# Layer 1's last two feed-forward chunks added straight to x, and four blocks of layer 2's input projection computed side by side

## The reference

```python
def rms_norm(x, w):
    xf = x.astype(F32)
    y = xf * lax.rsqrt(jnp.mean(xf * xf, axis=-1, keepdims=True) + EPS)
    return (y * w.astype(F32)).astype(x.dtype)

def modulate(h, shift, scale):
    return h * (1.0 + scale) + shift

def sq_relu_mlp(h, w1, w2):
    return jnp.square(jax.nn.relu(h @ w1)) @ w2          # w1 1024 x 4096, w2 4096 x 1024
...
        a_lat = modulate(rms_norm(h_lat, norm1_w[layer]), ml[0], ml[1])
        a_ctx = modulate(rms_norm(h_ctx, norm1_w[layer]), mc[0], mc[1])
...     # even_mixer in layer 0, odd_mixer in layer 1: it begins with a @ w_in, 1024 x 3104
        h_lat = h_lat + ml[2] * o_lat
        h_lat = h_lat + ml[5] * sq_relu_mlp(modulate(rms_norm(h_lat, norm2_w[layer]), ml[3], ml[4]),
                                            mlp_w1[layer], mlp_w2[layer])
        # and the same for h_ctx with mc where need_ctx
```

## Time and profile before

| | us |
|---|---|
| median of 3 runs (2121.18 to 2121.86) | 2121.32 |
| the profiled execution | 2117.72 |
| its span, first to last instruction | 2115.9 |
| TensorE busy with matmuls | 2023.8 (96%) |
| VectorE busy | 1547.1 (73%) |
| ScalarE busy | 913.4 (43%) |
| mean granted TensorE clock | 0.983 |

### The profile page before, as it was taken

How to read it: one execution, slowest core, us unless ns; L and a number is a source line. 1 busy time by engine, 2 the same in 40 slices (tenths; PEclk the granted TensorE clock), 3 DMA queues, 4 the chain that set the end, 5 groups by cost and what they waited for, 6 DMA issues and landing times. The chain is left out here.

```text
span 2115.9 us, 40356 instructions
## 1 busy us (share of the span) xinstructions
PE 2023.8 (96%) x16832; PEld 1782.8 (84%) x16832; DVE 1547.1 (73%) x2438; ACT 913.4 (43%) x1379; POOL 142.6 (7%) x231
## 2 busy tenths in 40 slices
PE   7999999999999999999999999999999999999997
PEld 5787777888888678789888999889899978989997
DVE  6875648899767668766646777789787777967555
ACT  2445553322222244422225544555654445655443
POOL 0100000010110001201220001000000100000000
PEclk7999999999999999999999999999999999999999
DMA  8542013455554176200003677443358844333552
GB/s 330 209 144 85 2 60 120 161 198 177 193 204 148 65 269 220 80 4 3 3 3 131 245 276 277 166 160 140 140 204 277 274 149 170 126 114 140 179 182 96
DMA packets 59135, 323.95 MB, mean 153 GB/s; under 512 B 6384, under 2 KB 7536, under 8 KB 32624
## 3 DMA queue, kind: packets, MB, share of 16 engines
q1 hardware_dynamic: 33360, 228.97, 30.3%
q0 software_dynamic: 25344, 92.29, 12.3%
q10 hardware_dynamic: 288, 0.66, 0.1%
HBM read 320.84 MB, written 1.05 MB: 152 GB/s over the span
## 5 line engine op out<-in xcount | busy, mean ns | idle before, releaser
L372 DVE TENSOR_TENSOR w_low<-raw,w_high 128x1024 fp32r<-128x1024 f32 (+1 forms) x408 | 475.4, 1202 | 151.1 <-ACT w_high L364 150.7
L364 ACT ACTIVATE w_high<-raw 128x1024 fp32r<-128x1024 f32 (+1 forms) x408 | 402.8, 1034 | 333.8 <-PE banks L409 322.6
L550 DVE SCALAR_TENSOR_TENSOR mod_rows<-mod_rows,silu_condition 128x1024 f32<-128x1024 f32 x162 | 196.0, 1221 | 2.6 <-ACT silu_condition L453 1.0
L407 PE MATMUL banks<-ffn_pre_scaled_l,w_high 128*128 128x258 f32 x640 | 180.6, 282 | 0.4 <-DVE w_low L372 0.4
L409 PE MATMUL banks<-ffn_pre_scaled_h,w_low 128*128 128x258 f32 x640 | 180.6, 282 | 0.0
L408 PE MATMUL banks<-ffn_pre_scaled_h,w_high 128*128 128x258 f32 x640 | 180.3, 282 | 0.0
L409 PE MATMUL banks<-mlp_hidden_h,w_low 128*128 128x512 f32 (+1 forms) x512 | 173.2, 338 | 0.0
L408 PE MATMUL banks<-mlp_hidden_h,w_high 128*128 128x512 f32 (+1 forms) x512 | 173.1, 338 | 0.0
L407 PE MATMUL banks<-mlp_hidden_l,w_high 128*128 128x512 f32 (+1 forms) x512 | 173.1, 338 | 0.0
L536 POOL DMA_DIRECT2D mod_rows<-rows_dram x162 | 86.1, 532 | 1238.5 <-DVE mod_rows L550 1045.0
L407 PE MATMUL banks<-mix_l,w_high 128*128 128x256 f32 (+1 forms) x448 | 129.5, 289 | 3.3 <-DVE w_low L372 2.3
(11 more groups left out here) (634 smaller groups left out, 5168.6 us busy)
## 6 DMA issues: line engine op xcount, KB each, us to landing
raw<-panels_dram SPq DMA_DIRECT2D x204, 1024.0 KB, 4.8
mod_rows<-rows_dram POOLq DMA_DIRECT2D x162, 512.0 KB, 5.3
mod_0a_rows<-rows_dram SPq DMA_DIRECT2D x8, 1024.0 KB, 19.4
odd_k_tok<-rows_dram POOLq DMA_DIRECT2D x14, 512.0 KB, 4.9
x_features<-x_features_dram SPq DMA_DIRECT2D x1, 2048.0 KB, 11.1
constants<-small_dram SPq DMA_DIRECT2D x1, 1672.5 KB, 6.6
silu_condition<-conditions_dram SPq DMA_DIRECT2D x2, 512.0 KB, 12.3
out_dram<-x_features SPq DMA_DIRECT2D x4, 256.0 KB, 2.1
```

The lines of the kernel that those rows point to most:

```text
L364: self.nc.scalar.activation(self.wh[:, m % 2, cols], self.raw[:, slot, cols], ACT.Copy).then_inc(self.w_high, 1)
L372: self.nc.vector.tensor_tensor(self.wl[:, m % 2, cols], self.raw[:, slot, cols], self.wh[:, m % 2, cols].bitcast(F32), ALU.subtract).then_ ...
L407: self.nc.tensor.matmul(out, sh(k), ml(k), start=(opens and k == 0), stop=False)
L550: nc.vector.scalar_tensor_tensor(row if v == nv - 1 else self.scratch[:], row, 1.0, self.cond[v][:], ALU.mult, ALU.mult, accum_out=mod[:, ...
```

## The change

Four edits.

1. `norm2_0`'s constant products behind the sums are 7 instead of 12.
2. In mlp0 (`direct`), when VectorE is at chunk 14 it first adds what y holds (chunks 0 to 13) to x, in 16 instructions, and then adds chunks 14 and 15 from PSUM to x, four instructions a group, in place of one addition to y. Behind each group of chunk 15 stand a half of the next panel's split (groups 0 and 1) and an addition of squares (groups 1 to 3). ScalarE squares each x block as soon as it is final. TensorE sums blocks 4, 5, the folded 0 to 3, 6 and 7: five sums for eight. The two constant products ahead of the sums go.
3. The second panel of layer 1 is split too before the block of code ends: on ScalarE between the squares and the root, on VectorE before the reciprocal.
4. In "odd_g" (`together=4`) the first four output blocks are computed side by side: for each operand block, 12 matmuls into four banks; the rest as before.

```diff
@@ def feed_forward(...)
+        def to_x(src, q, v):
+            x = self.xT[:, q, v * direct["half"]:(v + 1) * direct["half"]]
+            gate = direct["mod"][:, direct["gate"] + q, v:v + 1]
+            return nc.vector.scalar_tensor_tensor(x, src[:, v * direct["half"]:(v + 1) * direct["half"]], gate, x,
+                                                  ALU.mult, ALU.add)
+        def dve_begin_x(dve):
+            for w in direct["gates"]:
+                dve.wait_ge(*w)
+            dve.wait_ge(y_ready, 4 * (chunks - 2))
+            for g in range(4):
+                for q in (2 * g, 2 * g + 1):
+                    for v in range(direct["nv"]):
+                        last = to_x(y[:, q, :], q, v)
+            self.dve_chain.then(dve, last)
+        def dve_add_x(dve, cs, q=None, groups=range(4)):
+            for g in groups:
+                dve.wait_ge(down_done, cs * 4 + (g + 1))
+                if cs == chunks - 1:
+                    dve.wait_ge(y_ready, cs * 4 + (g - 3))
+                for o in (2 * g, 2 * g + 1):
+                    for v in range(direct["nv"]):
+                        last = to_x(ps[:, 4 + o % 4, 0:n], o, v)
+                    if o % 2:
+                        last.then_inc(y_ready, 1)
+                    elif cs == chunks - 1:
+                        last.then_inc(x_final, 1)
...
+                if direct is not None and which == "dve" and cs == chunks - 2:
+                    dve_begin_x(eng)
+                    add = dve_add_x
...
-            if not keep:
+            if direct is not None:
+                for g in range(4):
+                    dve_add_x(dve, chunks - 1, None, (g,))
+                    direct["between"](dve, g)
+            elif not keep:
                 dve_add(dve, chunks - 1)
@@ def odd_mixer(...)
-                        pr.copy_out(lambda q: gate[:, q, :]), a_ready, info=g_info, rising=True,
+                        pr.copy_out(lambda q: gate[:, q, :]), a_ready, info=g_info, rising=True, together=4,
@@ layer0
-                                           busy=(0, 12, 1), begun=...)
-                y, y_ready = pr.feed_forward("mlp0", D_FF // 256, False, n, high, low, a_ready, y, [], beside_mlp)
-                added = pr.add_feed_forward("mlp0", y, y_ready + outs[0], mod, 40, nv, n)
-                pr.next_norm(t, "norm1_1", n, lambda k: [(added[0][0], k + 1)], split=True, busy=(2, 4, 2))
+                                           busy=(0, 7, 1), begun=...)
+                def add_next(dve, q):
+                    dve.wait_ge(next_squared, q + 1)
+                    if q > 1:
+                        dve.wait_ge(next_folded, q - 1)
+                    nc.vector.tensor_tensor(next_squares[:, 0, :], next_squares[:, 0, :], next_squares[:, q, :],
+                                            ALU.add).then_inc(next_folded, 1)
+                def between(dve, g):
+                    if g < 2:
+                        pr.split_dve(dve, pr.m, parts=(g,))
+                        pr.split_next["dve"] = pr.m + g
+                    if g:
+                        add_next(dve, g)
+                _, x_done = pr.feed_forward("mlp0", D_FF // 256, False, n, high, low, a_ready, y, [], beside_mlp,
+                                            direct=dict(mod=mod, gate=40, nv=nv, half=n // nv, gates=outs[0],
+                                                        between=between))
+                @pr.block.scalar
+                def _(act):
+                    pr.split_upto("act", act, pr.m)
+                    for q in range(KD):
+                        for w in x_done(q):
+                            act.wait_ge(*w)
+                        nc.scalar.activation(next_squares[:, q, :], pr.xT[:, q, 0:n], ACT.Square).then_inc(next_squared, 1)
+                pr.next_norm(t, "norm1_1", n, [], split=True, splits=1, squares=next_squares, busy=(0, 4, 2),
+                             squared=(next_squared, (next_folded, 3), [4, 5, 0, 6, 7]))
```

More of the change, by code:

```diff
@@ L642, in rstd, with next_norm @@
         return r, squares, [(ready, 1)]
-    def next_norm(self, scope, name, n, ready, split=False, squares=None, busy=None):
+    def next_norm(self, scope, name, n, ready, split=False, squares=None, busy=None, squared=None, splits=0):
         return self.rstd(scope, name, self.xT[:, :, 0:n], ready, [list(range(KD))], n, D, self.c("ones"), 1, squares,
-                         r=self.next_rstd[:, :, 0:n], busy=busy,
-                         between=(lambda act: self.split_upto("act", act, self.m)) if split else None,
-                         meanwhile=(lambda dve, _: self.split_upto("dve", dve, self.m)) if split else None)
+                         r=self.next_rstd[:, :, 0:n], busy=busy, squared=squared,
+                         between=(lambda act: self.split_upto("act", act, self.m + splits)) if split else None,
+                         meanwhile=(lambda dve, _: self.split_upto("dve", dve, self.m + splits)) if split else None)
     def split_blocks(self, name, a, a_ready, high, low, counts=None):
@@ L978, in open_sums_first, with feed_forward @@
         self.block.tensor(lambda pe: self.open_sums(pe, banks))
-    def feed_forward(self, name, chunks, gated, n, high, low, a_ready, y, y_free, beside=None, wait_last=False, deferred=None):
+    def feed_forward(self, name, chunks, gated, n, high, low, a_ready, y, y_free, beside=None, wait_last=False, deferred=None,
+                     direct=None):
         nc = self.nc
@@ L1002, in feed_forward @@
         last_m = self.m - 1
-        bank_done = self.sem(f"{name}_bank_done")
+        bank_done = self.sem(f"{name}_bank_done") if keep else None
         tmp = ExitStack()
@@ L1240, in dve_add @@
                 ins.then_inc(y_ready, 1)
+        x_final = self.sem(f"{name}_x_final") if direct is not None else None
+        def to_x(src, q, v):
[24 more added lines that the diff above has]
+                        last.then_inc(x_final, 1)
         def turn(body, eng):
@@ L1258, in feed_forward, with step @@
         early = deferred is not None and gated
-        def step(which, up, high_or_low, add, rows=lambda eng, point: None):
+        def step(which, up, high_or_low, add_to, rows=lambda eng, point: None):
             def body(eng, cs, q):
+                add = add_to
                 if within and which == "dve" and q is None and cs == chunks - 2:
@@ L1387, in feed_forward @@
             return sums, lambda k: [(bank_done, k // 2 + 1) if k < 6 else (down_done, chunks)]
+        if direct is not None:
+            return None, lambda k: [(y_ready, 4 * (chunks - 1) + k // 2 + 1) if k % 2 else (x_final, k // 2 + 1)]
         return y, [(y_ready, 4 * chunks)]
@@ L3585, in layer0 @@
                     squares = pr.sb("norm2_0_squares", [P, KD, n], ctx=s)
+                with ExitStack() as s:
+                    next_squares = pr.sb("norm1_1_squares", [P, KD, n], ctx=s)
                 high = pr.sb("mlp0_a_h", [P, KD, n], F32R, ctx=t)
                 low = pr.sb("mlp0_a_l", [P, KD, n], F32R, ctx=t)
-                scaled, squared, folded, gain_ready = (pr.sem(f"norm2_0_{s}") for s in (
-                    "scaled", "squared", "squares_added", "gain_ready"))
+                scaled, squared, folded = (pr.sem(f"norm2_0_{s}") for s in ("scaled", "squared", "squares_added"))
                 x_info = {}
@@ L3618, in beside_out @@
                         eng.wait_ge(*rest_ready[0])
[L3619 to L3622, removed]
+                        pr.dve_chain.then(eng, nc.vector.scalar_tensor_tensor(
+                            gain[:], mod[:, 32:32 + KD, 0:nv], 1.0, spread(norm("norm2", 0), 2, nv), ALU.add, ALU.mult))
                         for q in range(4):
```

5 lines of the change are left out of this document (3 added, 2 removed).

## The result

| | before | changed kernel |
|---|---|---|
| median, us (range, runs) | 2121.59 (2121.18 to 2122.4, 4) | 2107.78 (2106.02 to 2108.92, 4) |
| ratio, 95% interval | | 0.9947, 0.9935 to 0.9958 |
| profiled execution, us (span) | 2117.72 (2115.9) | 2108.92 (2107.2) |

The forecast was 2110.0, range 2107.0 to 2114.0. The ratio is a gain of 11.2 us (8.9 to 13.8); the two medians lie 13.8 apart. The two profiled executions differ by 8.8 us.

What follows compares the result with a forecast made beforehand. TensorE, at 96% of the span, was taken as the bound, winnable only at the feed-forward's beginning and end. 2.85 + 5.45 + 4.65 - 1.7 = 11.25 us, taken off the median: 2110.0, range 2107.0 to 2114.0.

Steps and rivals of the forecast that it cites:

- rival (c): Gap opened ahead of mlp0's first product brings a low-clock spell: 2.85 becomes 1.15, total 2111.7; chance 0.07.
- rival (b): End of layer 1's feed-forward is worth less, by 1.5 (signals) or 2.1 (constant passes at half clock): 2112; chance 0.12.
- either late item: Before the reciprocal: TensorE's sums and the second panel's split, late together; each further 1 us on either is 1 us.
- B: Start of the first constant product in the block of code after layer 1's feed-forward; 737.2 us before, forecast 5.45 earlier.
- rival (a): The wait before block 4 (fifth output block) brings no low-clock spell: 2108.3; chance 0.20.
- (d): Transfers at the next block's start come some 3 us late at worst, delaying copy, third split and block 4: 2113; chance 0.05.
- (e): TensorE stays at half clock through the four blocks side by side and blocks 4 to 7: 9.85 slower, 2131.2; chance 0.02.

Runs made afterwards that it cites:

- the second execution of before: The kernel before once more, unchanged, for a second profile: profiled 2117.7 us.

## Why the prediction was right

**Edit 1** (2.85): 2.79, and 2.81 alone, and another 0.33 in the next stretch, so 3.1. The gap was 0.93 where I had 1.4. I took ten passes off 361.49, the start of the first product's record; but that record begins before the constant passes end, at 362.06 (351.60 and 10.46). Ten passes less is 357.8, and a gap of 0.9. No low clock stood behind it in any of the nine executions that have it, so rival (c) falls at this size of gap. The Trainium skill, "TensorE: Matmul & The Clock Gate", section "HAM oscillation — how this bites in real kernels", says that idle stretches between bursts bring the low clock back. The run without constant products agrees (6.94 idle, 6.8 at granted 0.58), the one with seven does not show it at 0.93.

**Edit 2** (5.45): 5.39 alone. From the last group to the reciprocal it took 5.91 where 5.95 was worked out, and the bank wait was 0.3 for 0.2. The chain of signals was counted right, so rival (b) falls. That each 1 us on either late item is 1 us was too strong for the split: without it the reciprocal came no earlier (5.92).

**Edits 3 and 4** (4.65, less 1.7 for a spell). Mis-sized a little: block 4 came at B+19.18 for B+19.6, since the constant passes ran at full clock and the operand was there at B+4.2, not 4.8; this was named as a bound (0.8 more), not as the value. The wait was 3.11 for 3.4 and the spell behind it cost 1.6 for 1.7. The reasoning on which that spell rested, that half clock follows because it followed a gap of this length before B and one ahead of 300 us, holds in some executions only: forecast and rival (a) are both true of this kernel, each in its executions. The forecast did not see that the gap before B itself would shrink, from 3.27 to 2.42, or that the spell there could go. Of the six executions with this wait of 3.1 five had the spell behind it (one of them with edits 3 and 4 alone), and one had not.

**Rivals (d) and (e).** Row product at 748.21 to 749.43, B+16.2, for B+16.0: the transfers were not late. The clock came back after each gap, at the latest after one low stretch.

**The time.** The steps sum to 12.0 (13.0 in the execution with the spell at B, each 0.5 less against the second execution of before), the forecast to 11.25, the ratio says 11.2 with 2.4 either way. That forecast and ratio meet within 0.1 is luck: the steps gave more than forecast, and the stretches outside them, which the forecast left at nothing, moved by -4.5 and +1.2 in the profiled pair. The median is 2.2 below the forecast's 2110.0: 0.75 to 1.75 of it may lie in the steps, the rest is within what the totals scatter.

## What to carry to other kernels

Where spells of low clock move a total by several us, compare the distance between two named instructions in both traces: where no low clock lies between them it repeats to 0.02 us, and it says which edit is worth what. Idle time of an engine is cover once only: VectorE's 6.25 us held the 16 additions at 0.3 us, and 5.4 us more work in the same place cost 6.3, of which 3.5 were waiting and the rest low clock that came with the wait. Before widening a pipeline (four blocks for two), look at what becomes late next: here a buffer that is read until the last step held the next panel back, and the second pair's gain was gone.

## What the runs showed of the hardware

Equal gaps of TensorE (2.42 us, and 3.11 us) were followed by the lower level in some executions of one kernel and not in others, and up to B these executions agreed to 0.01 us in every step from norm2_0 on. The same holds of the wait of 2.19 ahead of 300 us in two executions of the kernel before. What went differently lay further ahead: the first sum of norm2_0 started anywhere from 348.7 to 354.7 us behind code that all kernels share, with a wait near 142 us of 0.4 to 3.3 us and 0, 3.4 or 6.8 us of low clock behind it. The gap of 2.42 before B had low clock behind it in six executions and none in four. What decides it is open. The same addition to x costs 0.40 us in a row from PSUM (1.66 for 4) and from SBUF (6.42 for 16).
